# Key pages of a paged cache go to 64 adjacent partitions in four transfers of one strip each

## The reference

```python
past_k = cache_k[page_table].reshape(bs, -1, N_HEADS, HEAD_DIM)   # 8 x 32 pages of 128 x 16 x 64, float32
past_v = cache_v[page_table].reshape(bs, -1, N_HEADS, HEAD_DIM)

def stick_breaking_attention(q, k, v, bias, q_offset):
    ...
    z = jnp.einsum('bqhd,bkhd->bhqk', qb, kb) * scale + bias_f
    ...
    log_one_minus = jnp.where(causal, jax.nn.log_sigmoid(-z), 0.0)
    after = lax.cumsum(log_one_minus, axis=3, reverse=True) - log_one_minus
    w = jnp.where(causal, jnp.exp(jax.nn.log_sigmoid(z) + after), 0.0)
    o = jnp.einsum('bhqk,bkhd->bqhd', w, vb)
```

## Time and profile before

| | |
|---|---|
| time, median of 2 runs | 3479.67 us (3474.75 to 3484.59) |
| profiled execution, time | 3496.83 us |
| profiled execution, span | 3495.1 us |
| busy: PE, PEld, DVE, ACT, POOL | 2984.4, 2443.8, 1962.9, 1198.7, 375.6 us |
| DMA packets | 522242, 534.61 MB |
| mean granted clock of TensorE | 0.917 of full speed |

### The profile page before, as it was taken

The page is one execution under the profiler, slowest core; times in us unless marked ns, Lnnn a source line. Parts: engine busy times, 40 slices in busy tenths (PEclk is TensorE's granted clock), DMA queues, the critical chain, the costliest instruction groups (busy, mean ns, idle before and its releaser), DMA issues.

```text
span 3495.1 us, 57750 instructions
## 1 busy us (share of the span) xinstructions
PE 2984.4 (85%) x22468; PEld 2443.8 (70%) x22468; DVE 1962.9 (56%) x2764; ACT 1198.7 (34%) x2093; POOL 375.6 (11%) x588
## 2 busy tenths in 40 slices
PE   8999999999999999865555556566569999999999
PEld 7888888889999899633323323232248888899999
DVE  6997777456544553454444444554455776456532
ACT  5337433333333332332323223233234433333322
POOL 0220000000000121121212121222110000000000
PEclk9999999999999999987777677777789999999999
DMA  4332333333233564899999999999983333333232
GB/s 116 85 87 75 91 97 97 107 110 107 87 89 104 175 195 135 232 232 251 240 238 238 225 244 233 256 247 245 241 223 128 91 98 99 113 111 99 86 103 89
DMA packets 522242, 534.61 MB, mean 153 GB/s; under 512 B 28481, under 2 KB 406714, under 8 KB 521896
## 3 DMA queue, kind: packets, MB, share of 16 engines
q1 hardware_dynamic: 506262, 483.18, 53.9%
q0 software_dynamic: 15616, 47.55, 4.1%
q10 hardware_dynamic: 92, 0.19, 0.0%
HBM read 487.10 MB, written 33.89 MB: 149 GB/s over the span
## 4 chain that ended last, share of the span: by engine, by line
PE 57%; DMA 20%; DVE 9%; SPq 8%; issue 4%; ACT 2%; DVEq 0%; POOL 0%; ACTq 0%; POOLq 0%
PE PS L1150 52%; DMA kr<-in_cache_k 14%; DMA vr<-in_cache_v 5%; SPq L2205 4%; DVE mT L953 3%; DVE kt L2474 1%; SPq L2196 1%; SPq L2212 1%; DVE wlo L381 1%; PE PS L2265 1%; ACT whi L376 1%; PE PS L670 1%; PE PS L1801 0%; PE PS L1023 0%; PE PS L714 0%
## 5 line engine op out<-in xcount | busy, mean ns | idle before, releaser
L381 DVE TENSOR_TENSOR wlo<-raw,whi 128x1024 fp32r<-128x1024 f32 (+1 forms) x368 | 441.7, 1200 | 569.0 <-ACT whi L376 555.7
L376 ACT CAST whi<-raw 128x1024 fp32r<-128x1024 f32 (+1 forms) x368 | 379.4, 1031 | 935.2 <-PE PS L1150 891.1
L1150 PE MATMUL PS<-xfh,whi 128*128 128x512 f32 (+2 forms) x2240 | 619.0, 327 | 1.2 <-DVE wlo L381 0.9
L1150 PE MATMUL PS<-xfh,wlo 128*128 128x512 f32 (+2 forms) x2240 | 615.2, 326 | 0.0
L1150 PE MATMUL PS<-xfl,whi 128*128 128x512 f32 (+2 forms) x2240 | 613.6, 325 | 0.0
L2474 DVE STREAM_TRANSPOSE kt<-kr 128x1024 f32<-128x1024 f32 x256 | 309.3, 1227 | 516.0 <-DMA kr<-in_cache_k 508.7
L2288 PE MATMUL PS<-vr,wT 128*32 128x256 f32 x2048 | 202.9, 477 | 458.2 <-DMA vr<-in_cache_v 444.3
L2288 PEld LDWEIGHTS PS<-vr,wT 128*32 128x32 f32 x2048 | 47.1, 119 | 591.6 <-DMA vr<-in_cache_v 353.7
L1150 PEld LDWEIGHTS PS<-xfh,whi 128*128 128x128 f32 x2240 | 379.1, 188 | 35.9 <-issue 3.8
L1150 PEld LDWEIGHTS PS<-xfl,whi 128*128 128x128 f32 x2240 | 379.7, 188 | 32.2 <-issue 0.5
L1150 PEld LDWEIGHTS PS<-xfh,wlo 128*128 128x128 f32 x2240 | 378.5, 188 | 32.8
(11 more groups left out here) (366 smaller groups left out, 4972.7 us busy)
## 6 DMA issues: line engine op xcount, KB each, us to landing
kr<-in_cache_k SPq DMA_DIRECT2D x512, 256.0 KB, 11.9
vr<-in_cache_v SPq DMA_DIRECT2D x256, 512.0 KB, 18.9
raw<-in_ffn_w_gate SPq DMA_DIRECT2D x88, 512.0 KB, 3.7
raw<-in_ffn_w_up SPq DMA_DIRECT2D x88, 512.0 KB, 3.7
raw<-in_ffn_w_down SPq DMA_DIRECT2D x64, 512.0 KB, 3.5
raw<-in_ffn_w_down SPq DMA_DIRECT2D x32, 384.0 KB, 3.0
raw<-in_conv_w_glu SPq DMA_DIRECT2D x16, 512.0 KB, 4.2
raw<-in_conv_w_out SPq DMA_DIRECT2D x16, 512.0 KB, 3.5
```

Of the source, the lines that this page charges most:

```text
L376: nc.scalar.copy(whi[b][:, 0:blocks_of(t), :], raw[t % RAWS][:, 0:blocks_of(t), :]).then_inc(w_hi, 1)
L381: nc.vector.tensor_tensor(wlo[t % RAWS][:, 0:n, :], raw[t % RAWS][:, 0:n, :], whi[b][:, 0:n, :].bitcast(F32), ALU.subtract).then_inc(w_lo, 1)
L1150: mm = nc.tensor.matmul(PS[:, s + c, 0:c1 - c0], stationary(wt, t, kw + k), x(k0 + k)[:, c0:c1], start=start and k == 0 and wt is whi and ...
```

## The change

A page goes to partitions 64 z + 32 f + r, that is to 64 adjacent partitions, in four transfers of 128 KB, one for each strip c, where it went in two of 256 KB, one for each half f. The semaphore's target is 128 for each step, where it was 64. The rows of `kraw`, `qraw` and `qst` follow the new order of f and z. The transposes, the products and their counts stay.

```diff
@@ queries_placed
                 for q0 in range(4):
-                    f, z = q0 // 2, q0 % 2
+                    z, f = q0 // 2, q0 % 2
@@ smp_in_sp
                 for q0 in range(4):
-                    f = q0 // 2
+                    f = q0 % 2
@@ load_k_page
             page = A["cache_k"][ds(number, 1)].rearrange("a s h d -> (a s) (h d)")
-            for f in range(2):
-                q0 = 64 * f + 32 * z
-                sp.dma_start(kr[step % KT][q0:q0 + 32, :, :],
-                             page[:, 512 * f:512 * f + 512].rearrange("(c r) n -> r c n", c=4)).then_inc(s_k[step % KT], 16)
+            for c in range(4):
+                sp.dma_start(kr[step % KT][64 * z:64 * z + 64, c, :],
+                             page[32 * c:32 * c + 32, :].rearrange("r (f n) -> f r n", f=2)).then_inc(s_k[step % KT], 16)
@@ page_turned
                 if h == 0:
-                    dve.wait_ge(s_k[slot], 64 * (p // KT + 1))
+                    dve.wait_ge(s_k[slot], 128 * (p // KT + 1))
```

## The result

The changed kernel takes 5435.73 us (median of 2 runs, 5425.91 to 5445.54), the kernel before 3479.67. The ratio is 1.562, with an interval of 1.547 to 1.578: slower by more than half. The profiled execution has a span of 5443.8 us, 1948.7 more than before.

The account below looks back on a forecast made before the run. DMA bounds the attention stage (1200 us). With keys on two engines, 76.8 MB each at 22.2 GB/s makes 3459 us, 2259 more; added to 3496.8, less 17, 5739, so 5740 us predicted, range 5300 to 7370.

Parts of the forecast that it names:

- the rate of one engine: Attention stage: GB/s at which each of the two engines moves its 76.8 MB; 22.2 taken, bounds 15.1 and 25.4.
- the burst of key pages: Profile window 1402.0 to 1402.6 us before the change: 355 GB/s over 16 engines, 22.2 each, giving a 3459 us stage.
- my sum: Attention stage: two engines carry 67.1 MB of keys plus 9.7 MB of the rest each, 76.8 MB, in 3459 us.
- The row of 25.4: Profile window 1446 to 1450 us, mostly 4 KB rows: 25.4 GB/s for each engine, giving a stage of 3024 us.
- Rival 1: Key transfers still run on all 16 engines; only SP's issuing may cost: 3480 to 3560 us, chance 0.10.
- Rival 2: Two engines share a way into SBUF, 15.1 GB/s each: 7366 us; chance 0.22 for 6400 and above.
- Rival 3: Each key transfer runs on another pair of engines: 3480 to 4100 us, taken at 3750, chance 0.04.

Follow-up runs that it names:

- the run with two queues: Changed kernel, from the fourth step on strips 2 and 3 of a page issued by ScalarE from its own queue, the others by SP: 5412.67 us.
- the run with 16 engines: Changed kernel with the source of each key transfer walked with outer count 16, for its time alone: 3550.0 us, ratio 1.0168 to the kernel before.
- whole rows: Key page in one 512 KB transfer to all 128 partitions, 4 KB each, where the changed kernel has four; for its time alone: 3052.22 us.

## Why the prediction was right, and where it was off

**Right:** that the source's outer count of 2 puts a key transfer on two engines, read from 92 packets in 0.19 MB. The packets of q1 fell by 6144 as forecast, and counts of 4, 8 and 16 gave the packets and the order of times that this cause demands. Right too: that SP's issue order makes the 14 others wait, that the new placement changes no work on the computing engines, and that SP itself costs nothing beside this (0.512 us for an unheld issue, 4 of them within 12.3 us).

**Mis-sized:** the rate of one engine, the only factor of the sum. I took 22.2 GB/s from the burst of key pages; the measured one is 76.8 / 3150 = 24.4. At 24.4 the stage of my sum is 3150 instead of 3459 us, 309 less, and the miss is 5740 - 5436 = 304. That 24.4 comes out of the stage itself, but the packets give it too: 2048 bytes in 0.084 us. The reason I gave, that two engines are less disturbed than 16, held (0.084 us for a packet against 0.146). The row I took did not say what I read in it, as the burst by queue shows:

```profile
DMA packets 105, 0.21 MB, mean 355 GB/s; under 512 B 11, under 2 KB 11, under 8 KB 105
q1 hardware_dynamic: 96, 0.17, 93.5%
q0 software_dynamic: 9, 0.04, 23.1%
```

A fifth of its bytes were GpSimd's, in packets of over 4 KB. The 85 key packets alone are 0.174 MB in 0.6 us, 290 GB/s or 18.1 for each engine. Read rightly, the row would have put the time some 780 us further up (76.8 / 18.1 is 4243 us); that the forecast came within 304 us is in part luck. The row of 25.4, which I took as a bound, was the one to take. The DMA share came out at 0.29 where I expected 0.15 to 0.25: the key packets fill 0.115 of it, the packets of 4 KB 0.154, because they took 0.224 us on the mean and not the 0.159 of their median. My figure had no term for packets held up.

**Rival 1** (16 engines after all) fell with the packet count. Its price was tested all the same: with 16 engines the change costs 62 us (3550.0 against 3488.0), not the 30 of my estimate. The estimate let only the excess over 4.69 us for a page count, and took 4.8; the stage with 16 engines gives 4.92 for a page, an excess of 0.23 us, 59 us over 256 pages.

**Rival 2** (the two in each other's way) didn't happen: 24.4 GB/s for each, not 15.1. The port map of the Trainium skill (SBUF — State Buffer, section Door 1, the DMA port swizzle), by which partitions p and p + 32 share a port, led to an estimate of 7930 us; measured were 5436. The map itself is not refuted by this: if one engine runs some pieces ahead of the other, the two need not meet on one port. No run here tells whether that is so.

**Rival 3** (another pair each time) is excluded by the run with two queues. I had given it a bound of 4100 us by reasoning that work spreads; one queue that works off its transfers one by one could have given much the same stage (1024 x 65,536 bytes at 24.4 GB/s is 2750 us, and the value pages between them), and only the second queue, with its packet records, told them apart.

**Not seen ahead:** the placement costs 2% with the old cut (3566.9 against 3488.0), where I had given it no price. With the cut of the change no price of its own could be seen: it would lie within the 62 us of the run with 16 engines.

## What to carry to other kernels

Before a transfer is rearranged, read the outermost count of both its sides as they are written: the smaller one was the number of engines for 2, 4, 8 and 16, and a split that puts "2 halves" outermost puts a 512 KB page on two engines of 16, the same two for every such transfer of SP and ScalarE. In a profile it shows as low digits everywhere with SP held in its issues, and the packet count of the queue, less the pieces of data, gives the number of engines exactly. Where all engines are busy at 15 GB/s each, look at the destination: spreading consecutive transfers over partitions 64 apart, in the order in which they are issued, gave 0.85% for an exchange of two loops and a finer cut.

## What the runs showed of the hardware

- What an issue costs SP doesn't follow the number of engines. The least was 0.512 us for a key transfer on 2 engines, 0.537 on 4, 0.604 on 8 and 0.539 on 16, and 0.316 for 32 partitions on 16. But the load of the next page's number (line 2196) on SP took 0.452, 0.456 and 0.461 us at the median with 2, 4 and 8 engines, and 0.268 in every run in which all key transfers had 16.
- GpSimd's queue treats the same transfer differently. It added 136000 packets for 500 transfers, 272 for each, where SP's and ScalarE's queues take 66. The page counts 141337 packets under 512 bytes, where the changed kernel has 22337; with the 1000 completions that SP no longer leaves, that is 240 small packets for each transfer, so the 128 KB go in the other 32, of 4 KB each. An issue held GpSimd for 0.658 us at the median.
- TensorE's granted clock in the stage was 0.77 before, 0.58 after and 0.92 with whole rows: with longer waits for keys and values before its work it falls towards the lower level (1.2 of 2.4 GHz, 0.5), and its busy time in the stage grew from 725 to 866 us for the same products. No time of the kernel hung on it, since the waits were longer.
